# A two-layer block on one core: the last two pairs' down products in halves of 512 tokens, and a buffer of its own for the first weight sums

## The chip, the cores and the metric

One core of a Trainium2 chip runs the whole kernel. Its engines work side by side and meet only at semaphores: TensorE (PE, with its weight loads PEld) multiplies into the eight banks of PSUM, VectorE (DVE) and ScalarE (ACT) read and write PSUM and SBUF, GpSimd (POOL) works in SBUF, and SyncE (SP) starts transfers between SBUF and the chip's memory. The metric is the time of one execution in microseconds, as the median of several runs.

## The reference

Two transformer blocks over `x`, 1024 tokens of 1024 values, all in float32. The change lies in the last part of the second block and in the final norm:

```python
        x = x + merged @ w_out[l]
        h2 = rms_norm(x, norm2[l])
        x = x + jnp.square(jax.nn.relu(h2 @ w_up[l])) @ w_down[l]
    return rms_norm(x, final_norm)
```

`w_up` is 1024 x 4096 and `w_down` 4096 x 1024. `rms_norm` divides each token's values by the root of their mean square (plus 1e-6) and multiplies them by a gain.

## The kernel before

`X` holds the residual, turned: 128 partitions (values), 8 row groups of 128 values, 1024 tokens. A float32 product is made of three matmuls of 512 columns: each operand is split into an upper part (`hi`, rounded) and a rest (`lo`), and hi x hi, lo x hi and hi x lo are added in PSUM. The weights' split is POOL's: one operation makes the upper part by a product with one, a second the rest by subtraction, for 512 columns each (`split_to_slot`, lines 695 and 697).

The MLP runs over 16 pairs (`PAIRS_UP`), each of 256 hidden values. The up product of a pair is made of seven smaller products P1 to P7 over half of the tokens (a Strassen-like scheme: weight blocks and operands are added and subtracted before, results after). POOL makes the sums of weight blocks (`sums`, line 705 by way of `combine`): the sum of two blocks goes to `sum_up`, which lies where `h_hi` and `h_lo`, operands of the layer before, have been. Therefore `sums(0)` waits for `halves_done` at `2 * G_MLP`, the last product of that layer. The order in which POOL makes weights is written out in `W_ORDER`; weight number n goes to slot n mod 4, and POOL waits until the product that used the slot before has been done. After each weight `w_made` is raised by one.

TensorE's order at the start of the MLP is P1 of pair 0, P5 of pair 0, the mean square of `X` by token (`mean_square(4)`, line 797, a product with `mean_w`), P6 of pair 0, P2, P7, the spreading of the roots over the partitions (`spread_rms(4)`), P1 of pair 1, P4, P3, P6 and P5 of pair 1, then the down products of pair 0. SyncE loads pair 1's blocks of `w_up` (lines 562 and 565) once that mean has been made, since the sum of squares `sumsq_m` shares memory with them.

For a pair the hidden values are made in four blocks: VectorE applies relu and the root (`relu`, line 2177), ScalarE squares (line 1545) and makes the upper part (line 1550), VectorE makes the rest (line 2188, raising `hid_ready`). The down product of a pair has eight results q (row groups of `X`) of 1024 tokens: `down` issues 12 matmuls for each (lines 1101 to 1103), two banks wide, and VectorE adds the pair of banks to `X` (`add_down`, line 2200, raising `x_added`). Two pairs of banks alternate. Down weights are loaded in blocks of 256 KB, for two q of one pair each (`load_down`, line 572), into two buffers; a load waits for the split of the block two before it.

The last two pairs, 14 and 15, have their down products made together after the last up product. Each q takes 24 matmuls, those of pair 14 and of pair 15, after `hid_ready` of pair 15. For each q, ScalarE then squares `X` into `sq_f` (line 1194) and multiplies `X` by the final gain in place (line 1582), and VectorE adds the squares up in `sumsq_m` (lines 1614 and 1617). `sumsq_m` lies in memory of `up_1`; the first of these sums waits for the last weight of all, `w_made` at `len(W_ORDER)`:

```python
                if k == 0:
                    if n:
                        dve.wait_ge(w_made, len(W_ORDER))
                    dve.tensor_copy(sums[:], squares[:, 0]).then_inc(summed, 1)
```

VectorE's order there is `add_down(q)`, then the sum for q - 1. After the last q TensorE transposes `X` back to tokens x values (`turn_result`, line 1143, eight transposes for each of the eight blocks of 128 tokens), makes the mean square (`mean_square(5)`), ScalarE takes the root (line 1202), VectorE refines its inverse (lines 1644 to 1655), and VectorE (even blocks, line 2257) and ScalarE (odd blocks, line 1589) write the results, multiplied by the roots, to the four buffers of `y_out`. SyncE stores each block of 512 KB (line 587); a buffer is written again only when its store has been done.

## Time and profile before

| | us |
|---|---|
| median of 3 runs | 2008.71 |
| the runs, lowest and highest | 2003.52, 2009.34 |
| the profiled execution's own time | 2003.49 |
| its span, first to last instruction | 2001.7 |
| busy in it: PE, PEld | 1937.3, 1629.1 |
| busy in it: DVE, POOL, ACT | 942.0, 927.4, 618.9 |

The span is what all the rows count in; 1.8 us lie around it. A busy time says how long an engine had work in flight, not that it set the pace. A matmul's own duration is longer than its share: matmuls are pipelined, and the distance from one start to the next is what counts. "idle before" is the time that an engine stood still just before an instruction, with the instruction that released it.

### The profile page before, as it was taken

Reading aid. Unit: us, or ns where it says so; the run is one execution under the profiler, and the core shown is the slowest. Engines: PE = TensorE matmul, PEld = TensorE weight load, DVE = VectorE, ACT = ScalarE, POOL = GpSimd, SP = SyncE. Lnnn points to the kernel's source line nnn. Section 1 sums busy time; section 2 is a strip of 40 time slices with the busy share of each in tenths; the row PEclk is TensorE's granted clock in tenths of the full one; section 3 lists DMA queues with packets and bytes.
Section 4 is the critical chain, followed back from the end, with each engine's and each line's share of the span. In section 5 each row is a group of like instructions: output and inputs, shape, how many; then the busy total and the mean of one; then the engine's idle time right before and its main releaser. Section 6 shows DMA issues by size and latency. Waiting matters only on the chain.

```text
span 2001.7 us, 27035 instructions
## 1 busy us (share of the span) xinstructions
PE 1937.3 (97%) x9792; PEld 1629.1 (81%) x9792; DVE 942.0 (47%) x1682; ACT 618.9 (31%) x1154; POOL 927.4 (46%) x793
## 2 busy tenths in 40 slices
PE   7999999999999999999999999989999999999987
PEld 6778887788889888888888887878888888888876
DVE  5535554667545544454411216554444444444434
ACT  5025545546344544455300003331111111111123
POOL 4442227623222222112344444486777677776760
PEclk9999999999999999999999999999999999999998
DMA  4411012331111111110111113111121112111102
GB/s 127 106 43 32 27 38 85 87 126 40 41 40 41 30 48 43 32 33 22 32 47 47 48 52 126 58 64 43 44 72 53 43 43 74 53 43 43 53 32 84
DMA packets 145039, 109.85 MB, mean 55 GB/s; under 512 B 11273, under 2 KB 137745, under 8 KB 144929
## 3 DMA queue, kind: packets, MB, share of 16 engines
q1 hardware_dynamic: 132704, 89.67, 15.3%
q10 hardware_dynamic: 12224, 18.70, 3.0%
q8 instruction: 70, 1.15, 0.2%
q14 instruction: 41, 0.33, 0.1%
HBM read 99.91 MB, written 11.59 MB: 56 GB/s over the span
## 4 chain that ended last, share of the span: by engine, by line
PE 87%; DVE 6%; issue 2%; ACT 2%; POOL 1%; DMA 1%; SPq 0%; POOLq 0%; DVEq 0%; ACTq 0%
PE ps L773 12%; PE ps L774 12%; PE ps L775 12%; PE ps L897 6%; PE ps L1101 6%; PE ps L1102 6%; PE ps L1103 6%; PE ps L1062 5%; PE ps L1064 5%; PE ps L1063 5%; PE ps L886 3%; PE ps L872 2%; PE ps L867 1%; PE ps L819 1%; PE ps L821 1%
## 5 line engine op out<-in xcount | busy, mean ns | idle before, releaser
L633 POOL TENSOR_TENSOR w_hi<-raw,ones 128x512 fp32r<-128x512 f32 x146 | 163.7, 1121 | 810.2 <-PE ps L775 794.1
L773 PE MATMUL ps<-h_hi,w_hi 128*128 128x512 f32 x1024 | 407.7, 398 | 12.4 <-DVE tmp L1675 3.4
L774 PE MATMUL ps<-h_lo,w_hi 128*128 128x512 f32 x1024 | 401.5, 392 | 0.0
L775 PE MATMUL ps<-h_hi,w_lo 128*128 128x512 f32 x1024 | 400.8, 391 | 0.0
L2200 DVE TENSOR_TENSOR X<-ps,X 128x1024 f32<-128x1024 f32 x120 | 146.9, 1224 | 230.3 <-PE ps L1103 230.3
L773 PEld LDWEIGHTS ps<-h_hi,w_hi 128*128 128x128 f32 x1024 | 193.7, 189 | 50.8 <-DVE tmp L1675 5.9
L775 PEld LDWEIGHTS ps<-h_hi,w_lo 128*128 128x128 f32 x1024 | 193.2, 189 | 42.1
L774 PEld LDWEIGHTS ps<-h_lo,w_hi 128*128 128x128 f32 x1024 | 193.7, 189 | 34.5 <-issue 0.7
L1101 PE MATMUL ps<-hid_hi,slot_hi 128*128 128x512 f32 x512 | 201.0, 392 | 10.3 <-DVE X L2200 6.8
L637 POOL TENSOR_TENSOR w_lo<-raw,w_hi 128x512 fp32r<-128x512 f32 x146 | 200.8, 1375 | 11.4
L1102 PE MATMUL ps<-hid_lo,slot_hi 128*128 128x512 f32 x512 | 200.4, 391 | 0.0
L1103 PE MATMUL ps<-hid_hi,slot_lo 128*128 128x512 f32 x512 | 200.1, 391 | 0.0
L1545 ACT ACTIVATE ps<-ps 128x512 f32<-128x512 f32 x64 | 37.2, 582 | 515.5 <-DVE ps L2177 515.4
L695 POOL TENSOR_TENSOR slot_hi<-up,ones 128x512 fp32r<-128x512 f32 x96 | 99.9, 1041 | 124.2 <-PE ps L1103 115.8
L897 PEld LDWEIGHTS ps<-v_seq,probs_t 128*128 128x128 f32 x1056 | 136.8, 191 | 15.5 <-DVE o_seq L1747 3.0
L1247 ACT ACTIVATE probs<-probs,least 128x640 f32<-128x640 f32 (+7 forms) x128 | 94.2, 736 | 137.9 <-DVE least L1736 137.6
L897 PE MATMUL ps<-v_seq,probs_t 128*128 128x64 f32 x1056 | 132.2, 269 | 3.1 <-DVE o_seq L1747 1.5
L697 POOL TENSOR_TENSOR slot_lo<-up,slot_hi 128x512 fp32r<-128x512 f32 x96 | 123.8, 1289 | 7.5
L1101 PEld LDWEIGHTS ps<-hid_hi,slot_hi 128*128 128x128 f32 x512 | 96.9, 189 | 31.4 <-DVE X L2200 7.3
L1256 ACT ACTIVATE probs_t<-ps 128x512 f32<-128x512 f32 (+2 forms) x192 | 81.6, 460 | 105.2 <-PE ps L886 104.2
L1103 PEld LDWEIGHTS ps<-hid_hi,slot_lo 128*128 128x128 f32 x512 | 96.9, 189 | 20.3
L1102 PEld LDWEIGHTS ps<-hid_lo,slot_hi 128*128 128x128 f32 x512 | 97.0, 189 | 20.1
(300 smaller groups left out, 3624.3 us busy)
## 6 DMA issues: line engine op xcount, KB each, us to landing
raw<-in_w_in SPq DMA_DIRECT2D x116, 256.0 KB, 2.9
up<-in_w_up SPq DMA_DIRECT2D x32, 512.0 KB, 3.9
down_raw<-in_w_down SPq DMA_DIRECT2D x64, 256.0 KB, 3.4
raw<-in_w_out SPq DMA_DIRECT2D x32, 256.0 KB, 2.8
x_in<-in_x SPq DMA_DIRECT2D x8, 512.0 KB, 7.8
raw_b<-in_w_out SPq DMA_DIRECT2D x16, 256.0 KB, 2.9
x_store<-X ACTq DMA_DIRECT2D x8, 512.0 KB, 2.8
bias_fox<-c_rows ACTq DMA_DIRECT2D x8, 512.0 KB, 4.4
```

The costliest lines, as they stand in the source:

```text
L633: pool.tensor_tensor(w_hi[:, half].rearrange("p k n -> p (k n)"), raw[:, half].rearrange("p k n -> p (k n)"), f32(ones[:, 0:1]).broadcast_ ...
L637: pool.tensor_tensor(w_lo[:, half], raw[:, half], f32(w_hi[:, half]), ALU.subtract).then_inc(weights_split, 1)
L697: pool.tensor_tensor(lo, src, f32(hi), ALU.subtract).then_inc(w_made, 1)
L773: pe.matmul(o, w1, hi[:, k, c], start=first, stop=False)
L774: pe.matmul(o, w1, lo[:, k, c], start=False, stop=False)
L775: mm = pe.matmul(o, w2, hi[:, k, c], start=False, stop=last)
L897: mm = pe.matmul(bank(2, HD), buf["probs_t"][:, (g + gi) % 4, b * P:(b + 1) * P], buf["v"][st][:, kb + b, head * HD:(head + 1) * HD], star ...
L1062: pe.matmul(o, hi[:, k], b_hi[:, k], start=first and k == 0, stop=False, skip_group_check=not first)
L1101: pe.matmul(o, w1, hid[0][:, k, c], start=first and k == 0, stop=False)
L1102: pe.matmul(o, w1, hid[1][:, k, c], start=False, stop=False)
L1103: mm = pe.matmul(o, w2, hid[0][:, k, c], start=False, stop=last and k == 1)
L2200: dve.tensor_tensor(X[:, q], pair(q % 2), X[:, q], ALU.add).then_inc(x_added, 1)
```

## The change

It has two parts.

The start: POOL's sum of two weight blocks for pair 0 goes to `sum_up_0`, memory of its own, and `sums(0)` no longer waits for the last product of the layer before. The upper parts of four weights, P7 of pair 0, P1 of pair 1, P7 and P4 of pair 15, are made by ScalarE (`split_hi`) and not by POOL, which still makes the rests.

The end: the down products of pairs 14 and 15 are made over 512 tokens at a time (`tail`), first all eight q for tokens 0 to 511 (h = 0), then for 512 to 1023 (h = 1), in the order of `tail_order`: three products of pair 14, the same three of pair 15, then both pairs by turns. Each q of a half has one bank. The down weights of both pairs are loaded and split a second time for the second half (blocks E0 to E3). Squares go to a PSUM bank, sums to `sumsq_m`, by halves; the first of them waits for P3 of pair 15. The first half's mean, root, transposes (blocks 0 to 3), scaling and store stand between the second half's products in each engine's order. `y_out` has eight buffers and no waits for a store.

```diff
-    return order + [(f"D{j}", i) for j in range(4) for i in (PAIRS_UP - 2, PAIRS_UP - 1)]
+    a, b = PAIRS_UP - 2, PAIRS_UP - 1
+    order += [("D0", a), ("D1", a), ("D0", b), ("D1", b)]
+    order += [(f"D{j}", i) for j in (2, 3) for i in (a, b)]
+    return order + [(f"E{j}", i) for j in range(4) for i in (a, b)]
+def tail_order():
+    a, b = PAIRS_UP - 2, PAIRS_UP - 1
+    order = [(0, q, i) for i in (a, b) for q in range(3)]
+    order += [(0, q, i) for q in range(3, 8) for i in (a, b)]
+    return order + [(1, q, i) for q in range(8) for i in (a, b)]
+DOWNS = 8 * (PAIRS_UP - 2)
+TAIL_BANK = ((4, 5, 7, 6, 4, 5, 7, 6), (4, 5, 4, 5, 4, 5, 4, 5))
+TAIL_SQUARE = (0, 7)
+TAIL_MEAN = 6
+TURN_PAIR = (0, 1, 0, 1, 0, 1, 2, 3)
+ACT_HI = [("P7", 0), ("P1", 1), ("P7", PAIRS_UP - 1), ("P4", PAIRS_UP - 1)]
+def slot_free(name, i):
+    j = int(name[1])
+    return T_AT[int(name[0] == "E"), 2 * j + 1, i] + 1
+    sum_up_0 = z_at("sum_up_0", W_SLOT, F32, 100)
-    y_out = t_at("y_out", [P, 4, D], F32, 0)
+    y_out = t_at("y_out", [P, NB, D], F32, 0)
...
+                    elif i >= PAIRS_UP - 2:
+                        pool.wait_ge(tail_done, slot_free(name, i))
...
+                if op in ACT_HI:
+                    pool.wait_ge(act_hi_made, ACT_HI.index(op) + 1)
+                else:
+                    pool.tensor_tensor(hi, src, one, ALU.mult).then_inc(slot_hi_made, 1)
+                    pool.wait_ge(slot_hi_made, pool_hi_at(op))
                 pool.tensor_tensor(lo, src, f32(hi), ALU.subtract).then_inc(w_made, 1)
...
-                if i == 0:
-                    pool.wait_ge(halves_done, 2 * G_MLP)
-                combine(sum_up[:], block(i, 2, 1), block(i, 2, 2), ALU.add)
+                total_up = sum_up if i else sum_up_0
+                combine(total_up[:], block(i, 2, 1), block(i, 2, 2), ALU.add)
...
+            def tail(h, q, i):
+                n = W_AT[f"{'DE'[h]}{q // 2}", i]
...
+                last = i + 1 == PAIRS_UP
+                hid, c, o = hid_t[last], (N1, N2)[h], bank(TAIL_BANK[h][q])
+                pe.wait_ge(w_made, n + 1)
+                if last and h == 0 and q == 0:
+                    pe.wait_ge(hid_ready, 4 * PAIRS_UP)
+                if not last:
+                    if h == 0 and q == 0:
+                        pe.wait_ge(r_made, 4 * (PAIRS_UP - 2) + 1)
+                    elif h == 0 and q == 1:
+                        pe.wait_ge(r_made, 4 * (PAIRS_UP - 1) + 1)
+                    elif h == 0 and q == 2:
+                        pe.wait_ge(d_read, 3 * PAIRS_UP)
+                    elif h == 0 and q == 3:
+                        pe.wait_ge(c_read, 2 * PAIRS_UP)
+                    elif h == 0:
+                        pe.wait_ge(x_added, DOWNS + q - 3)
+                    elif q < 2:
+                        pe.wait_ge(x_added, DOWNS + 5 + q)
+                    else:
+                        pe.wait_ge(x_added, DOWNS + 8 + q - 1)
+                for k in range(2):
+                    w1, w2 = hi[:, k, q % 2], lo[:, k, q % 2]
+                    pe.matmul(o, w1, hid[0][:, k, c], start=not last and k == 0, stop=False, skip_group_check=True)
+                    pe.matmul(o, w1, hid[1][:, k, c], start=False, stop=False, skip_group_check=True)
+                    mm = pe.matmul(o, w2, hid[0][:, k, c], start=False, stop=last and k == 1, skip_group_check=True)
+                mm.then_inc(tail_done, 1)
+            def turn_result(i, ks):
+                h = i // 4
+                pe.wait_ge(x_gained, 8 * h + ks[-1] + 1)
+                if i in (2, 3, 4, 5):
+                    pe.wait_ge(y_made[i % 2], (i - 2) // 2 + 1)
...
+            for h, q, i in TAIL:
+                tail(h, q, i)
+                if (h, i) == (1, PAIRS_UP - 1):
+                    if q == 0:
+                        mean_tail(0)
+                    elif 1 <= q <= 4:
+                        turn_result(q - 1, range(KT))
+                    elif q == 6:
+                        turn_result(4, range(6))
+                        turn_result(5, range(6))
+            turn_result(4, [6])
+            turn_result(5, [6])
+            turn_result(4, [7])
+            mean_tail(1)
+            turn_result(5, [7])
+            turn_result(6, range(KT))
+            pe.wait_ge(mean_read, 2)
+            turn_result(7, range(KT))
...
             keep_first(0)
+            act.wait_ge(w_made, W_AT["P6", 0] + 1)
+            split_hi(("P7", 0), up_1[0][:, :, P:2 * P])
+            act.wait_ge(up_1_loaded[1], 16)
+            split_hi(("P1", 1), up_1[1][:, :, 0:P])
...
+            for h in range(2):
+                c = (N1, N2)[h]
+                for q in range(KT):
+                    act.wait_ge(x_added, DOWNS + 8 * h + q + 1)
+                    if q:
+                        act.wait_ge(f_summed, 8 * h + q)
+                    act.activation(bank(TAIL_SQUARE[h]), X[:, q, c], ACT.Square).then_inc(f_squared, 1)
+                    act.activation(X[:, q, c], X[:, q, c], ACT.Copy, scale=gains[:, 4, q:q + 1]).then_inc(x_gained, 1)
...
+                    if h and q in (2, 4):
+                        turn_out(q - 1)
...
+            for h in range(2):
+                for q in range(KT):
+                    add_tail(h, q)
+                    sum_tail(h, q)
+                    if h and q == 0:
+                        root_tail(0)
+                    if h and q in (1, 3):
+                        turn_out(q - 1)
+            root_tail(1)
+            turn_out(4)
+            turn_out(6)
```

`add_tail` adds one bank to 512 tokens of `X`, `sum_tail` adds a bank of squares to `sumsq_m`, `root_tail` is the refinement for four blocks, and `mean_tail` the product with `mean_w` for four. `turn_out(i)` scales block i into `y_out`, on VectorE for even i and on ScalarE for odd. ScalarE makes the two upper parts of pair 15 after the hidden values of pair 14.

## Rows read from the trace of the kernel before

**Rows 1.** The page: busy time, share and instructions of each engine.

```profile
PE 1937.3 (97%) x9792; PEld 1629.1 (81%) x9792; DVE 942.0 (47%) x1682; ACT 618.9 (31%) x1154; POOL 927.4 (46%) x793
```

**Rows 2.** TensorE's waits, 1300 to 2002: waiter <- releaser: total us, times, longest.

```profile
PE ps L1101 <- DVE X L2200: 6.8, 1, 6.8
PE ps L1062 <- POOL slot_lo L697: 5.9, 2, 4.3
PE ps L1101 <- DVE hid_lo L2188: 3.5, 1, 3.5
```

**Rows 3.** Busy time by stage: us, busy (x instructions) by engine, clock, DMA.

```profile
1339.00:1895.00 556.00, 556.00 (x2455) 460.38 (x2454) 249.72 (x282) 67.69 (x117) 413.28 (x353) 1.00 0.16 52
```

**Rows 4.** TensorE's timeline, 1304 to 1335: start, us, instruction, [idle before <-releaser].

```profile
1304.35 0.39 PE L1064 MATMUL ps<-b_hi,slot_lo 128*128 128x512 f32 x1
1309.03 0.80 PE L1062 MATMUL ps<-t_hi,slot_hi 128*128 128x512 f32 x1 [4.30 <-POOL slot_lo L697]
...
1334.08 0.47 PE L1062 MATMUL ps<-t_hi,slot_hi 128*128 128x512 f32 x1 [1.63 <-POOL slot_lo L697]
```

**Rows 5.** POOL's timeline, 1302 to 1309, same columns.

```profile
1302.19 1.29 POOL L705 TENSOR_TENSOR sum_up<-up,up 128x512 f32<-128x512 f32 x1 [3.06 <-PE ps L775]
...
1307.71 1.26 POOL L697 TENSOR_TENSOR slot_lo<-sum_up,slot_hi 128x512 fp32r<-128x512 f32 x1
```

**Rows 6.** The chain that ended last, 1309 to 1320: start us, us, what.

```profile
1309.83 0.43 PE ps L1063
...
1313.38 1.69 PE ps L797 x16
...
1315.09 3.79 DMA up<-in_w_up
```

**Rows 7.** VectorE's and ScalarE's timelines, 1294 to 1308.

```profile
1294.17 0.74 DVE L2116 SCALAR_TENSOR_TENSOR b_lo<-X,gains,b_hi 128x512 fp32r<-128x512 f32 x1
...
1305.24 1.50 DVE L2127 SCALAR_TENSOR_TENSOR b_lo<-X,gains,b_hi 128x512 fp32r<-128x512 f32 x1
...
1307.92 0.68 DVE L2102 TENSOR_TENSOR sumsq_m<-ps,sumsq_m 128x512 f32<-128x512 f32 x1
...
1303.38 0.72 ACT L1522 ACTIVATE b_hi<-X,gains 128x512 fp32r<-128x512 f32 x1 [5.84 <-DVE X L2109]
```

**Rows 8.** The page: groups of POOL's splits, busy us, mean ns | idle before.

```profile
L695 POOL TENSOR_TENSOR slot_hi<-up,ones 128x512 fp32r<-128x512 f32 x96 | 99.9, 1041 | 124.2 <-PE ps L1103 115.8
...
L697 POOL TENSOR_TENSOR slot_lo<-up,slot_hi 128x512 fp32r<-128x512 f32 x96 | 123.8, 1289 | 7.5
```

**Rows 9.** TensorE's, then VectorE's timeline, 1925 to 1957.

```profile
1926.46 0.79 PE L1101 MATMUL ps<-hid_hi,slot_hi 128*128 128x512 f32 x1 [3.49 <-DVE hid_lo L2188]
...
1956.88 0.80 PE L1101 MATMUL ps<-hid_hi,slot_hi 128*128 128x512 f32 x1 [6.84 <-DVE X L2200]
...
1955.00 0.69 DVE L1614 COPY sumsq_m<-sq_f 128x1024 f32<-128x1024 f32 x1 [14.58 <-POOL slot_lo L697]
```

**Rows 10.** Line 572's loads, issue to landing: all 64, then the last six.

```profile
DMA to landing us min/median/max: 2.5/3.4/6.4
...
DMA to landing us min/median/max: 2.5/2.6/2.8
```

**Rows 11.** The chain that ended last, 1980 to 1991.

```profile
1980.63 1.24 DVE X L2200
...
1984.59 1.74 PE ps L797 x16
...
1987.91 2.49 DVE y_out L2257 x2
```

**Rows 12.** DMA engines' busy tenths in 40 slices of 1985 to 2002.

```profile
DMA  0000000000019999999999999999999999992000
```

**Rows 13.** Busy time by stage, in two stretches of transposes.

```profile
1980.60:1984.00 3.40, 2.51 (x21) 2.03 (x19) 3.26 (x3) 2.10 (x2) 0.00 (x0) 1.00 0.00 0
1989.20:1995.60 6.40, 6.29 (x32) 6.05 (x32) 3.40 (x3) 1.94 (x2) 0.00 (x0) 0.58 0.88 351
```

More of the change, by code:

```diff
@@ L581, in _ @@
                         load_down(4 * (i - 1) + j)
-            for n in range(4 * (PAIRS_UP - 2), 4 * PAIRS_UP):
+            for n in range(4 * (PAIRS_UP - 2), len(D_ORDER)):
                 load_down(n)
@@ L724, in _ @@
             sums(0)
-            split_to_slot(("P5", 0), sum_up[:])
+            split_to_slot(("P5", 0), sum_up_0[:])
             split_to_slot(("P6", 0), block(0, 1, 1))
@@ L1087, in first_of_c, with down @@
                 product("P5", i, BANK_C)
-            def down(q, i, hid, first=True, last=True):
+            def down(q, i):
                 n = W_AT[f"D{q // 2}", i]
@@ L1100, in down @@
                         o = bank(2 * (q % 2) + b)
-                        pe.matmul(o, w1, hid[0][:, k, c], start=first and k == 0, stop=False)
-                        pe.matmul(o, w1, hid[1][:, k, c], start=False, stop=False)
-                        mm = pe.matmul(o, w2, hid[0][:, k, c], start=False, stop=last and k == 1)
-                if last:
-                    mm.then_inc(down_done, 1)
+                        pe.matmul(o, w1, hid_t[0][0][:, k, c], start=k == 0, stop=False)
+                        pe.matmul(o, w1, hid_t[0][1][:, k, c], start=False, stop=False)
@@ new lines, in mean_tail @@
+            def mean_tail(h):
+                pe.wait_ge(f_summed, 8 * h + 8)
+                if h:
+                    pe.wait_ge(mean_read, 1)
+                for i in range(4):
+                    b = 4 * h + i
+                    mm = pe.matmul(ps[:, TAIL_MEAN, i:i + 1], sumsq_m[:, b * P:(b + 1) * P], mean_w[:],
+                                   start=True, stop=True)
+                mm.then_inc(mean_done, 1)
+            def turn_result(i, ks):
[3 more added lines that the diff above has]
+                    pe.wait_ge(y_made[i % 2], (i - 2) // 2 + 1)
+                for k in ks:
+                    mm = pe.transpose(ps[:, 2 * TURN_PAIR[i] + k // 4, (k % 4) * P:(k % 4 + 1) * P],
+                                      X[:, k, i * P:(i + 1) * P], ident[:])
+                if ks[-1] == KT - 1:
+                    mm.then_inc(y_turned, 1)
@@ new lines, in root_tail @@
+            def root_tail(h):
+                dve.wait_ge(root_made, 6 + h)
+                ms, root, y, t = (rms[:, n, 4 * h:4 * h + 4] for n in range(4))
+                dve.tensor_scalar(ms, bank(TAIL_MEAN, 4), EPS, None, ALU.add).then_inc(mean_read, 1)
+                dve.wait_ge(mean_read, h + 1)
+                step(dve.reciprocal(y, root))
+                step(dve.tensor_tensor(t, ms, y, ALU.mult))
+                step(dve.tensor_tensor(t, t, y, ALU.mult))
+                step(dve.tensor_scalar(t, t, -0.5, 1.5, ALU.mult, ALU.add))
+                dve.tensor_tensor(y, y, t, ALU.mult).then_inc(scale_ready, 1)
```

138 lines of the change are left out of this document (61 added, 77 removed).

## The prediction

> **What bounds the kernel now.** I read the page first, then TensorE's waits, then the busy table by stages, then each stall's neighbourhood in the timelines and the chain. On the page TensorE is busy for 1937.3 us of the span of 2001.7 us [rows 1], so the change can only win back part of some 64 us and can't make the products shorter. The reader should see in the list of waits that in the last 700 us only three of TensorE's waits are large: 6.8 us on an addition into `X`, 5.9 us on POOL's `slot_lo` (two waits, the longer 4.3) and 3.5 us on `hid_lo` [rows 2]. Between 1339 and 1895 us TensorE is busy for all of 556.00 us, 2455 matmuls at 0.2265 us each [rows 3]: whatever is won before 1339 us is carried unchanged to 1895, and nothing in between can give or take. So two stretches count: the start of the MLP (1302 to 1339) and its end (from 1923). After the last product, at 1980.6, another 21.1 us pass to the span's end [rows 11], in which TensorE only turns results and makes the mean.
>
> **Start of the MLP.** P1 of pair 0 issues its last matmul at 1304.35 and ends 0.23 later, at 1304.6; P5 begins at 1309.03 [rows 4]. It waited for POOL: from the end of P1's split, 1302.19 - 3.06 = 1299.1, POOL idled until the last product of the layer before was done, since `sum_up` lies in `h`'s memory, and only then made three sums and P5's split, 1302.19 to 1308.97 [rows 5]. With `sum_up_0` elsewhere the sums start at 1299.15; the same 6.8 us of work end at 1305.95 (the splits' slots are free at 1302.0, before they are wanted). P5 starts 3.1 us earlier. After the wait of 4.3 us matmuls came 0.43 apart instead of 0.23, the lower of the two clock levels (1.2 against 2.4 GHz), for seven of them [rows 4, 6]: 7 x 0.2 = 1.4 us. After a wait of only 1.63 us the first matmul took 0.47 against 0.80, and the clock had not fallen [rows 4]; the wait that is left is 1.35 us, so the 1.4 us go too. P5 ends at 1308.8, and the mean's sums (last addition 1307.92 + 0.68, [rows 7]) are just ready, so the mean begins 4.6 us earlier than at 1313.38 [rows 6]. What is late next is the load of pair 1, which waits for that mean: 1315.09, landing 3.8 us later, then POOL works without a pause until P6 of pair 1 can begin, at 1334.08 [rows 4, 6]. That chain moves by the 4.6, and by 0.4 more, since ScalarE makes P1's upper half (0.72 for 512 columns [rows 7]) where POOL takes 1.04 and a gap [rows 8]. ScalarE's two new copies stand in front of the `b22` tops, and the first waits there for pair 1's load: tops from 1315.0, the second `b22` rest at about 1318.2, wanted by TensorE at 1318.7. That cover is thin, but a later landing moves POOL's chain by as much, so it is paid once. TensorE reaches P6 of pair 1 at about 1327.9 and starts at 1329.0: **5.0 us won**. Bounds: 3.1 (only the first wait goes) and 5.9 + 1.4 = 7.3 (both waits and the slow clock go whole).
>
> Here a rule speaks against the change. First the row: a VectorE operation with `X` and `b_hi` (both in SBUF) took 1.50 us at 1305.24 with POOL at work, while a like one took 0.74 at 1294.17 without [rows 7]. The Trainium skill (SBUF — State Buffer, Who interferes with whom) states that a VectorE instruction with two SBUF inputs and a GpSimd instruction that reads SBUF exclude one another for their whole length; the trace agrees. By it, POOL's splits moved under VectorE's last operands could hold the mean's sums for one POOL operation, 1.3 us, and the start would gain 3.7 in place of 5.0.
>
> **The end: the wait for the last hidden values.** TensorE ends P3 of pair 15 at 1926.46 - 3.49 = 1923.0 and idles for `hid_lo` [rows 9]. Now three products of pair 14 (18 matmuls, 4.1 us) need no value of pair 15 and fill 1923.0 to 1927.1, past `hid_lo`'s 1926.4. Their banks 4, 5 and 7 are free by 1921. Won: 3.5, and the slow clock after it: its first matmul took 0.79 as at 1309.03 [rows 4, 9], and with eight at 0.2 more that is 1.6. The first block's split is ready in time: POOL gives two upper halves to ScalarE, idle there, and is 2.2 us earlier.
>
> **The end: VectorE behind POOL.** The copy that begins `sumsq_m` waited 14.58 us until POOL had read the last weights, and the addition for the third product stood behind it in VectorE's queue; TensorE idled 6.84 us and restarted at the low clock (first matmul 0.80, again eight) [rows 9]. The new sum waits only for P3 of pair 15. Won: 6.8 + 1.6 = 8.4. The 192 matmuls stay 192, each still with its own weights, at 0.2265 [rows 3]: 43.5 us.
>
> **What is added there.** Eight more loads of 256 KB and eight more splits on POOL. A split is 1.04 + 1.29 and gaps, 2.36 [rows 8]; a load of the last six landed in 2.5 to 2.8 us [rows 10], and waits for the split two before it. So two splits cost 2.65 + 2.36 = 5.0 us and feed 24 matmuls of pairs 14 and 15, 5.4 us: hidden, barely. Following slots block by block, the smallest reserve is 0.4 us (product 4 of the first half) and 0.8 (product 6). At 3.4 us each, the median of all 64 loads, the same reckoning gives 0.3 us of stalls, at 4.0 us 1.5, and at 6.4 us, the largest, 13.9 [rows 10]. I take none: those of over 3 us ran beside loads of `up`, of which none is left here. VectorE adds, ScalarE squares and VectorE sums a product's half in 3 x 0.7 = 2.1 us [rows 7] while TensorE takes 2.72, or 3.8 with a turn: hidden, the first root and four output scalings (1.24 each [rows 11]) too; without that cover each costs its length. Beside the second half TensorE also does 44 transposes (21 took 2.5 [rows 13]: 5.3 us), half of the mean (1.7 / 2 = 0.9 [rows 6]) and six changes of kind and back, estimated at 0.8 from the 0.47 against 0.39 of a first matmul [rows 4]: **7.0 us added on the path**. SyncE issues the stores behind the last loads, about 1955, when the first result is ready; nothing waits for it.
>
> **After the last product.** Before: addition, square, scaling, last transposes, mean (1.74, to 1986.3), root (1.6, to 1987.9), output scaling [rows 11], and eight stores, whose bytes fill 24.5 of the 40 slices of 0.425 us, 10.4 us one behind the other [rows 12]: 21.1 us in all. Now on half the columns: addition, square and sum 0.7 each, last transpose and mean 1.1, root 1.5, first scaling 1.3: 6.0 us to the first of four stores. Then some 0.9 to the first bytes, half of 10.4 = 5.2, and 0.9 to the span's end [rows 12]: 13.0. Won: 8.1.
>
> **Sum.** TensorE's last product ends at 1923.0 + 43.5 + 7.0 = 1973.5 and the span at 1986.5, with the old start; 15.2 us won (by parts 5.1 + 8.4 + 8.1 - 7.0 = 14.6). With the start's 5.0: 20.2. The span becomes 1981.5, an execution like the profiled one 2003.5 - 20.2 = 1983.3. The runs shown spread from 2003.5 to 2009.3 with the median at 2008.7, 5.2 above the profiled one; the same shift on the median gives 1988.5. I take the middle, **1986 us**.
>
> **Rivals.**
> *The start is held by something else* (0.12): VectorE shut out by POOL, or ScalarE held at pair 1's load in front of the `b22` tops. For it speaks the 1.50 us above; against, that the sums are wanted only at 1308.8. Gain 3.1 to 3.7 there: 1988.
> *The weight feed runs late* (0.12): loads land in 4 us rather than 2.6. It speaks for it that the reserve is 0.4 us, against it that the six loads without company took 2.6 [rows 10]. 1.5 us of stalls, up to 3 with a slow restart: 1988 to 1989.
> *Turning locks TensorE to the copies* (0.1): results 2 to 5 reuse two pairs of banks and wait for an output scaling of 1.24 us [rows 11]. Each scaling stands behind an addition and a sum in VectorE's queue; if all four waits last one scaling, 5 us: 1991. Against it, a product and its turn give VectorE 3.8 us.
> *It doesn't overlap* (0.04): a wait that I misread keeps the first half's norm behind the second half; then the 8.1 and part of the 8.4 stay unearned and 7.0 is added: 1999 to 2006.
> *Slower: the clock* (0.03). Between 1989.2 and 1995.6 TensorE did 32 transposes with the granted clock at 0.58 [rows 13]. If turns between products drop the second half to the low level, each matmul costs 0.2 us more; 20.2 / 0.2 = 101 matmuls is where the change turns slower, and only the second half's 96 with some of the mean and turns beside them reach it: 2009 to 2012. Against it: 21 transposes between 1980.6 and 1984.0 with short idle left it at 1.00 [rows 13]. The Trainium skill (TensorE: Matmul & The Clock Gate, Loop structure matters more than you think) warns of waits between matmuls that send the clock down; by it turns with nothing idle around them should be harmless, and rows 13 agree.
>
> **How the numbers follow.** Forecast 0.59, the rest as given. A measurement tells 0.3%, 6 us, from no change. Faster holds the forecast, the first three rivals and a little of the fourth: 0.93; same 0.04; slower 0.03. The range goes from 1979 (both waits at the start gone whole, executions like the profiled one, and a shorter end) to 1997 (turning and feed together on the median): 8 in 10.
>
> **What would show it.** P5 of pair 0 starts 1.3 us after P1 and P6 of pair 1 about 5 us earlier. From P3 of pair 15 to the last product about 50.5 us (before 57.6), with no wait over 1 us and a clock near 1.00; from it to the end about 13 (before 21.1). A stall before product 4 or 6 of the first half names the feed; matmuls 0.43 apart name the clock. I am wrong if the stretch 1339 to 1895 has changed, or if POOL, not TensorE, ends the first half.

## The result, and the profile after

| | before | after |
|---|---|---|
| median of 4 runs each, us | 2007.63 | 1985.9 |
| the runs, lowest and highest | 2003.52, 2009.34 | 1985.52, 1987.36 |
| the profiled execution's own time | 2003.49 | 1987.36 |
| its span | 2001.7 | 1985.6 |

The ratio of after to before is 0.9896, with a 95% interval from 0.9879 to 0.9913: the change makes the kernel 21.7 us faster. The forecast was 1986.

TensorE's waits of the changed kernel, from 1290 us to the end (waiter, releaser, total us, times, longest), answer to [rows 2]:

```profile
PE ps L1094 <- POOL slot_lo L730: 2.3, 2, 1.2
PE ps L1188 <- ACT X L1683: 1.8, 1, 1.8
PE ps L1094 <- DVE u_t L2249: 0.8, 1, 0.8
```

The waits of 6.8 us on the addition into `X` and of 3.5 us on `hid_lo` are gone, and the 5.9 us on `slot_lo` are 2.3. What is left are 1.10 us before P5 of pair 0 and 1.22 us before P6 of pair 1. New is 1.8 us behind the last product, where TensorE turns the last values; the 0.8 us on `u_t` stood in before too. TensorE's timeline at these places, which answers to [rows 4], and POOL's, which answers to [rows 5]:

```profile
1310.08 0.50 PE L1094 MATMUL ps<-t_hi,slot_hi 128*128 128x512 f32 x1 [1.10 <-POOL slot_lo L730]
...
1333.39 0.47 PE L1094 MATMUL ps<-t_hi,slot_hi 128*128 128x512 f32 x1 [1.22 <-POOL slot_lo L730]
```

```profile
1302.09 1.29 POOL L730 TENSOR_TENSOR slot_lo<-up,slot_hi 128x512 fp32r<-128x512 f32 x1
1303.52 1.29 POOL L738 TENSOR_TENSOR sum_up<-up,up 128x512 f32<-128x512 f32 x1
...
1308.76 1.27 POOL L730 TENSOR_TENSOR slot_lo<-sum_up,slot_hi 128x512 fp32r<-128x512 f32 x1
1309.98 1.49 POOL L728 TENSOR_TENSOR slot_hi<-up,ones 128x512 fp32r<-128x512 f32 x1
```

POOL's first sum follows the split of P1 by 0.1 us; before, POOL stood still for 3.06 us there. Neither wait brought the clock down: the first matmuls took 0.50 and 0.47 us and those behind them came 0.23 apart. The table by stretches (us, then busy time and instructions of PE, PEld, DVE, ACT, POOL, then the granted clock, the DMA share and GB/s) has the middle of the MLP, the start, the second half's products, and the turns behind the last product:

```profile
1339.00:1890.00 551.00, 551.00 (x2433) 456.39 (x2432) 248.38 (x280) 67.80 (x117) 410.11 (x349) 1.00 0.16 52
1310.00:1316.00 6.00, 5.92 (x34) 5.20 (x35) 4.63 (x11) 1.99 (x6) 5.04 (x5) 1.00 0.03 8
1947.10:1972.00 24.90, 24.90 (x136) 21.04 (x136) 14.55 (x23) 10.88 (x17) 11.58 (x10) 1.00 0.35 128
1975.70:1979.60 3.90, 3.76 (x18) 3.36 (x17) 3.33 (x8) 1.42 (x3) 0.00 (x0) 0.50 0.06 23
```

The middle is what it was [rows 3]: busy for all of its 551.00 us, 2433 matmuls at 0.2265 us. The second half's products and the turns between them keep TensorE busy for all of 24.90 us at a clock of 1.00.

Since the middle can't change, each kernel below is read by three distances: from the start of P1 of pair 0 to the end of P3 of pair 15 (start and middle), from there to the end of the last down product (the tail), and from there to the span's end. The first two kernels:

```
                       P1 at     P1 to P3   tail    behind it   their sum
before                 1301.85   620.96     57.62   21.27       699.85
after                  1306.10   616.03     49.66   13.81       679.50
```

The changed part is 4.9 + 8.0 + 7.5 = 20.4 us shorter, and the span only 16.1, because this execution reached P1 of pair 0 4.25 us later than that of before. Up to there both kernels run the same code. 2.8 of the 4.25 us come from the first 60 us (same columns as above, first before, then after):

```profile
0.00:60.00 60.00, 48.15 (x220) 39.87 (x221) 35.47 (x45) 29.66 (x37) 26.21 (x42) 0.94 0.42 121
```

```profile
0.00:60.00 60.00, 47.22 (x208) 39.20 (x209) 32.31 (x42) 29.61 (x37) 22.61 (x41) 0.89 0.38 111
```

While the first inputs land, after got through 208 matmuls and before through 220, with a granted clock of 0.89 against 0.94. The other 1.4 us arise between 304 and 447 us. Over the fourteen profiled executions of this study P1 of pair 0 began between 1300.28 and 1306.10 us. Whole runs scatter by about as much; where only the order of work at the start or the end of the MLP differs, the three distances say more than the medians.

### The profile page after: what moved, and what is told of

Read it like the earlier page. It is cut to its first block, busy times and chain, and to the rows that moved or that the text cites. A ratio compares the mean times of both kernels' runs of the same rounds, so it can differ in the third digit from the quotient of the medians.

```text
span 1985.6 us, 27160 instructions
## 1 busy us (share of the span) xinstructions
PE 1935.4 (97%) x9792; PEld 1628.3 (82%) x9792; DVE 947.4 (48%) x1704; ACT 624.3 (31%) x1175; POOL 942.5 (47%) x805
## 3 DMA queue, kind: packets, MB, share of 16 engines
q1 hardware_dynamic: 134880, 91.77, 15.8%
## 4 chain that ended last, share of the span: by engine, by line
PE 89%; DVE 6%; issue 2%; ACT 2%; POOL 1%; DMA 0%; SPq 0%; DVEq 0%; ACTq 0%; POOLq 0%
PE ps L805 12%; PE ps L806 12%; PE ps L807 12%; PE ps L929 6%; PE ps L1135 5%; PE ps L1133 5%; PE ps L1134 5%; PE ps L1094 5%; PE ps L1096 5%; PE ps L1095 5%; PE ps L918 3%; PE ps L904 2%; PE ps L851 1%; PE ps L899 1%; PE ps L853 1%
## 5 line engine op out<-in xcount | busy, mean ns | idle before, releaser
L2292 DVE TENSOR_TENSOR X<-ps,X 128x1024 f32<-128x1024 f32 x112 | 137.2, 1225 | 205.3 <-PE ps L1135 205.3
L1133 PE MATMUL ps<-hid_hi,slot_hi 128*128 128x512 f32 x448 | 174.3, 389 | 0.0
L1134 PE MATMUL ps<-hid_lo,slot_hi 128*128 128x512 f32 x448 | 174.3, 389 | 0.0
L1135 PE MATMUL ps<-hid_hi,slot_lo 128*128 128x512 f32 x448 | 174.3, 389 | 0.0
L730 POOL TENSOR_TENSOR slot_lo<-up,slot_hi 128x512 fp32r<-128x512 f32 x96 | 123.7, 1290 | 10.0 <-ACT slot_hi L1643 2.8
L1835 DVE RECIPROCAL inv_total<-total 128x1 f32<-128x1 f32 x192 | 31.4, 163 | 154.1 <-PE ps L929 152.2
L1094 PE MATMUL ps<-t_hi,slot_hi 128*128 128x512 f32 x256 | 100.0, 391 | 3.1 <-POOL slot_lo L730 2.3
L1095 PE MATMUL ps<-t_lo,slot_hi 128*128 128x512 f32 x256 | 99.6, 389 | 0.0
```

The source lines that it names most:

```text
L1094: pe.matmul(o, hi[:, k], b_hi[:, k], start=first and k == 0, stop=False, skip_group_check=not first)
L1095: pe.matmul(o, hi[:, k], b_lo[:, k], start=False, stop=False, skip_group_check=not first)
L1133: pe.matmul(o, w1, hid_t[0][0][:, k, c], start=k == 0, stop=False)
L1134: pe.matmul(o, w1, hid_t[0][1][:, k, c], start=False, stop=False)
L1135: mm = pe.matmul(o, w2, hid_t[0][0][:, k, c], start=False, stop=k == 1)
L2292: dve.tensor_tensor(X[:, q], pair(q % 2), X[:, q], ALU.add).then_inc(x_added, 1)
```

## The experiments

None of these kernels leaves work out. Distances in us come from one profiled execution each, medians from the runs; "won" means against before.

### The start alone

The changes at the start, put into the kernel before:

```diff
-                if i == 0:
-                    pool.wait_ge(halves_done, 2 * G_MLP)
-                combine(sum_up[:], block(i, 2, 1), block(i, 2, 2), ALU.add)
+                total_up = sum_up if i else sum_up_0
+                combine(total_up[:], block(i, 2, 1), block(i, 2, 2), ALU.add)
...
+ACT_HI = [("P7", 0), ("P1", 1)]
```

> The kernel before with the start of the change alone: sum_up_0, and the upper parts of P7 of pair 0 and P1 of pair 1 by ScalarE. Theory (TensorE's path through sums, mean, load of pair 1 and POOL): from P1's last matmul of pair 0 to P6 of pair 1 it takes 24.5 us where before took 29.7, so 5.0 us less than before in all, 2002.6 where before is 2007.6. Rival (VectorE shut out by POOL, or ScalarE held at the load): 3.1 to 3.7 us less. The second wait, before P6 of pair 1, about 1.2 us by the theory.

Measured: 2002.29 us (1999.3 to 2003.87), ratio 0.9974 [0.9965, 0.9984]. The distances are 616.10, 58.13 and 21.28. The start won 4.86 us, as in the whole change (4.93), and nothing behind it gave any of it back: the two waits of the tail are still 3.49 and 6.85 us.

What did change is the price of the clock behind the wait of 3.49 us. TensorE's timeline of this kernel (start, us, instruction, idle before):

```profile
1925.54 0.50 PE L1114 MATMUL ps<-hid_hi,slot_hi 128*128 128x512 f32 x1 [3.49 <-DVE hid_lo L2211]
...
1926.12 0.41 PE L1116 MATMUL ps<-hid_hi,slot_lo 128*128 128x512 f32 x1
1926.34 0.61 PE L1114 MATMUL ps<-hid_hi,slot_hi 128*128 128x512 f32 x1
1926.76 0.63 PE L1115 MATMUL ps<-hid_lo,slot_hi 128*128 128x512 f32 x1
```

In before the first matmul behind that wait was already slow, 0.79 us [rows 9]. Here, behind the same wait, the first four start 0.34, 0.24 and 0.22 us apart, and only then do they come 0.42 apart.

Without ScalarE's two copies, with `sum_up_0` alone:

> The kernel before with sum_up_0 alone; POOL makes all upper parts. Theory: the first wait falls from 4.3 to about 1.1 us and the slow clock goes; the mean moves by 4.6 us and the load of pair 1 with it, so 4.6 us less than before, and the wait before P6 of pair 1 is 1.5 us. Rival (ScalarE's two copies carry more than 0.4 us of the start's gain): 3 us or less.

Measured: 2002.67 us (1999.41 to 2005.08), ratio 0.9982 [0.9972, 0.9991]; 616.33, 59.15 and 21.31. Its waits at the start, and those of the kernel with the copies:

```profile
PE ps L1062 <- POOL slot_lo L698: 2.6, 2, 1.5
```

```profile
PE ps L1075 <- POOL slot_lo L711: 2.4, 2, 1.3
```

The buffer is worth 4.6 us, ScalarE's copies 0.23 us more. The medians of the two kernels, 0.4 us apart with runs over some 5 us, can't tell them apart; the waits, 1.53 and 1.28 us before P6 of pair 1, can.

### One wait of the end

The kernel before, with only the wait in front of the first sum of squares changed:

```diff
-                        dve.wait_ge(w_made, len(W_ORDER))
+                        dve.wait_ge(w_made, W_AT["P3", PAIRS_UP - 1] + 1)
```

> The kernel before with one wait changed: the first sum of squares waits for P3 of pair 15 and no longer for the last weight. The down products keep their 1024 tokens. Theory: the wait of 6.8 us goes and with it the slow restart, 8.4 us less than before; the wait of 3.5 us for hid_lo stays, POOL's splits are ready 3 us or more before they are wanted. Rival (the next wait in line takes its place, a split that waits for its slot): 3 to 5 us less, with a wait of 3 us or more on slot_lo.

Measured: 1997.38 us (1996.1 to 1998.68), ratio 0.9957 [0.994, 0.9973]. The distances are 622.56, 47.31 and 21.29. One line in VectorE's queue shortens the tail by 10.3 us. TensorE's waits and its restart:

```profile
PE ps L1062 <- POOL slot_lo L697: 6.0, 2, 4.3
PE ps L1101 <- DVE hid_lo L2188: 3.5, 1, 3.5
```

```profile
1929.35 0.50 PE L1101 MATMUL ps<-hid_hi,slot_hi 128*128 128x512 f32 x1 [3.49 <-DVE hid_lo L2188]
1929.68 0.39 PE L1102 MATMUL ps<-hid_lo,slot_hi 128*128 128x512 f32 x1
1929.92 0.39 PE L1103 MATMUL ps<-hid_hi,slot_lo 128*128 128x512 f32 x1
```

The 6.84 us are gone with what followed them, and this time the other wait, of the same 3.49 us, cost no clock at all: the tail is 47.31 = 43.5 (192 matmuls) + 3.49 + 0.3. The 0.3 is what a restart costs even at full clock. By the same subtraction before paid 57.62 - 43.5 - 10.33 = 3.8 us for two restarts, the start alone 4.3 and the buffer alone 5.3; less 0.3 for each restart, the two low clocks cost 3.2, 3.7 and 4.7.

At the start this kernel has the old wait of 4.3 us. Its windows behind that wait and over the tail, and the window of before behind its own:

```profile
1310.30:1318.00 7.70, 7.68 (x29) 6.52 (x30) 1.10 (x2) 0.07 (x1) 6.78 (x6) 0.59 0.01 3
1925.80:1973.00 47.20, 43.71 (x193) 36.11 (x193) 17.51 (x17) 15.94 (x17) 15.28 (x12) 1.00 0.09 29
```

```profile
1309.00:1315.10 6.10, 6.07 (x29) 5.26 (x30) 1.11 (x2) 0.01 (x1) 5.87 (x6) 0.76 0.01 4
```

The same 29 matmuls took 6.1 us in before and 7.7 us here: the clock stayed low for all twelve matmuls of P5 and part of the mean, where in before it came back after seven. `end_only`, below, is like this one. So the execution from which the prediction was made had a mild low clock at the start, and 620.96 is the smallest of the three values with that wait.

### The end alone

The whole change at the end, with the old `sum_up`, its wait, and no copies at the start:

```diff
-ACT_HI = [("P7", 0), ("P1", 1), ("P7", PAIRS_UP - 1), ("P4", PAIRS_UP - 1)]
+ACT_HI = [("P7", PAIRS_UP - 1), ("P4", PAIRS_UP - 1)]
...
+                if i == 0:
+                    pool.wait_ge(halves_done, 2 * G_MLP)
```

> The changed kernel with the start as before: sum_up and its wait, POOL makes the upper parts of pair 0 and of P1 of pair 1. Theory: the two parts of the change don't touch each other, so the end alone is worth the whole less the start: 15.2 us by the sum, 15 to 17 by the measured whole of 21.7 less 5. The stretch from P3 of pair 15 to the last product takes 49.7 us as in the changed kernel. Rival (the parts share a gain): 19 us or more.

Measured: 1990.42 us (1986.95 to 1992.65), ratio 0.9916 [0.9898, 0.9934]; 622.20, 49.66 and 13.41. The tail is to the hundredth that of the whole change, so the parts don't touch each other. From P3 of pair 15 to the span's end it takes 63.1 us where before took 78.9: the end alone is worth 15.8. Against this kernel the start is worth 622.20 - 616.03 = 6.2 us.

### How much are the halves worth?

`one_wait` is one line; the halves with their second feed, norm and stores are most of the diff. The start (as in the first kernel) and that one line (as in the third) together, still with 1024 tokens to a product:

> The kernel before with the start of the change and the one changed wait, 1024 tokens at a time. Theory: 5.0 + 8.4 = 13.4 us less than before, so that the halves of 512 tokens with all that goes with them are worth the other 7 to 8. Rival: if the halves only serve to take that wait away, this kernel is as fast as the changed one, 21 us less.

Measured: 1991.75 us (1990.38 to 1992.98), ratio 0.9925 [0.9908, 0.9941]; 616.11, 48.95 and 21.32, in sum 686.4. The whole change has 679.5. So of its 20.4 us the start gives 4.9, the one line 8.7 to 10.3, depending on the clock behind the other wait, and the halves the last 6.9. In the tail the halves are even longer (49.66 against 48.95, with the 3.5 us of wait filled and the turns added); they earn their part behind the last product, where half of the norm and of the stores is left.

### Turns between the products, or behind them

Turns and stores of the first half's blocks moved behind the last product, and with them the twelve turns of blocks 4 and 5; the sums, the mean and the root of the first half are left where they are:

```diff
-                    elif 1 <= q <= 4:
-                        turn_result(q - 1, range(KT))
-                    elif q == 6:
-                        turn_result(4, range(6))
-                        turn_result(5, range(6))
```

> The changed kernel with the first half's four turns, scalings and stores moved behind the last product; its sums and its root stay beside the second half. Theory (what is beside the products costs TensorE 4.1 us there and takes the same from the end, since eight stores at 10.4 us then set the end): within 2 us of the changed kernel either way; the last product ends 4 us earlier, and 17 to 18 us follow it instead of 13.6. Rival (the hidden stores are what the halves bring): 5 us slower or more.

Measured: 1984.15 us (1983.78 to 1985.38), ratio 0.9889 [0.9873, 0.9906]; 616.00, 44.70 and 16.26. The tail lost 4.96 us and the rest grew by 2.45 against after: in sum 677.0 against 679.5. The 44 transposes with their changes of kind cost 0.113 us each on TensorE's path, near the 0.12 of [rows 13]; what they bring is less. Behind the last product it was forecast that 17 to 18 us would follow, and 16.3 did. The transfers of this kernel from 1966 to 1983 (busy share of the DMA engines in 40 slices of 0.425 us, tenths):

```profile
DMA  0000000000799999999999999999999999800000
```

and those of after from 1969 to 1986:

```profile
DMA  0000000000000000000000005999999999996000
```

Eight stores take 25 slices, 10.6 us, and four take 13, 5.5 us. But in after the first bytes leave 7.4 us behind the last product and here 4.2 us; these first stores need nothing of the second norm. 5.1 us more of transfers, less 3.2 us of earlier start, and some 0.5 between them and the span's ends make the 2.45; the turns had cost twice that. The medians of the two kernels can't tell them apart (the intervals overlap), the distances do: with `after_again` (679.0, below) the gain is 2.0 us, with after 2.5.

Only the twelve turns of the second half's own blocks moved, from beside product 6 to behind the loop:

```diff
-                    elif q == 6:
-                        turn_result(4, range(6))
-                        turn_result(5, range(6))
+            turn_result(4, range(6))
+            turn_result(5, range(6))
```

> The changed kernel with twelve transposes of blocks 4 and 5 moved from before the last product to behind it, where TensorE waits 1.8 us for the last scaled values. Theory: 1.3 to 1.5 us less than the changed kernel, the last product ends that much earlier and still 13.6 us follow it. Rival (they delay the last transposes and the mean): no change, or up to 0.5 us more.

Measured: 1981.37 us (1980.11 to 1983.94), ratio 0.9878 [0.9861, 0.9894]; 616.18, 48.31 and 13.16. The tail is 1.35 us shorter and the rest doesn't grow: these turns fit into the 1.84 us for which TensorE waits there for the last values.

The same, with the squares' sums in memory of `rstd` instead of `up_1`, so that pair 1's load waits for no mean:

```diff
-    sumsq_m = z_at("sumsq_m", [P, S], F32, 102)
+    sumsq_m = rstd
...
-                    sp.wait_ge(mean_done, 5)
```

The first of those sums then waits for the last root of pair 15 (`r_made`) and no longer for P3.

> As turn_in_gap, and the sum of squares lies in rstd's memory instead of in that of up_1, so the load of pair 1 no longer waits for the mean. Theory: the wait of 1.2 us before P6 of pair 1 goes, since POOL's splits no longer wait for that load; 2.4 to 2.7 us less than the changed kernel. Rival (POOL is the bound there anyway, or a new wait of ScalarE): the 1.2 us stay, and it equals turn_in_gap.

Measured: 1983.4 us (1981.27 to 1983.99), ratio 0.9881 [0.9864, 0.9897]; 614.64, 48.31 and 13.22. TensorE's waits:

```profile
PE ps L1093 <- POOL slot_lo L729: 1.1, 1, 1.1
PE ps L1093 <- DVE u_t L2247: 0.8, 1, 0.8
PE ps L1187 <- ACT X L1681: 0.5, 1, 0.5
```

The wait before P6 of pair 1 is gone and 1.5 us with it. Pair 1's load was issued 0.2 us after P1 of pair 0 began, and 8.7 us after it in the changed kernel, so the mean held that load, as the prediction said. The median is not below that of the kernel before it (1981.37); this execution reached P1 of pair 0 at 1305.83 and the other at 1300.75, and by the distances it is 676.2 against 677.7.

### The order of the first products

Pairs 14 and 15 by turns from the start, without the three products of pair 14 in front:

```diff
-    order = [(0, q, i) for i in (a, b) for q in range(3)]
-    order += [(0, q, i) for q in range(3, 8) for i in (a, b)]
+    order = [(0, q, i) for q in range(8) for i in (a, b)]
```

> The changed kernel with the first half's products in plain turns, pair 14 then pair 15 for each q, and not three of pair 14 first. Theory: TensorE waits for hid_lo after one product instead of none: 3.5 - 1.4 = 2.1 us of wait, and no slow clock after so short a wait, so 2.1 us more on the way from P3 of pair 15 to the last product (49.7). Rival (the clock falls as after 3.5 us): 3.7 us more.

Measured: one run, 1988.22 us (before beside it: 2007.85); 616.08, 52.21 and 13.20. The timeline:

```profile
1924.73 0.47 PE L1164 MATMUL ps<-hid_hi,slot_hi 128*128 128x512 f32 x1 [2.23 <-DVE hid_lo L2279]
1925.04 0.40 PE L1165 MATMUL ps<-hid_lo,slot_hi 128*128 128x512 f32 x1
```

One product of pair 14, six matmuls or 1.36 us, still stands in front, and 3.49 less 1.36 is about the 2.23 of this wait. The tail is 2.55 us longer by it, and after it the clock did not fall.

### How thin is the weight feed?

One more POOL operation, a sum of `sum_up` with itself, before the split that product 4 of the first half wants:

```diff
+                if D_ORDER[n] == ("D2", PAIRS_UP - 1):
+                    pool.wait_ge(tail_done, slot_free("D1", PAIRS_UP - 2))
+                    combine(sum_up[:], sum_up[:], sum_up[:], ALU.add)
```

> The changed kernel with one more POOL operation of 1.3 us just before the split of block D2 of pair 15, on which product 4 of the first half waits. Theory (that reserve is 0.1 to 0.4 us): a wait of 1.0 to 1.3 us on slot_lo before the second part of product 4, of which nothing is caught up: the way from P3 of pair 15 to the last product grows from 49.7 by about 1.1 us. Rival (the reserve is larger than it looks, since TensorE's queue runs ahead): no wait.

Measured: one run, 1986.94 us; 616.08, 50.69 and 13.25. Its waits:

```profile
PE ps L1097 <- POOL slot_lo L730: 2.4, 2, 1.3
PE ps L1191 <- ACT X L1686: 1.8, 1, 1.8
PE ps L1168 <- POOL slot_lo L730: 0.9, 1, 0.9
```

The added sum and the second part of product 4 in the timelines:

```profile
1931.02 1.04 POOL L738 TENSOR_TENSOR sum_up<-sum_up 128x512 f32<-128x512 f32 x1 [4.33 <-PE ps L1170]
...
1934.58 0.50 PE L1168 MATMUL ps<-hid_hi,slot_hi 128*128 128x512 f32 x1 [0.93 <-POOL slot_lo L730]
```

The same place in the changed kernel as it is:

```profile
1933.08 1.30 POOL L730 TENSOR_TENSOR slot_lo<-down_raw,slot_hi 128x512 fp32r<-128x512 f32 x1
...
1934.14 0.39 PE L1167 MATMUL ps<-hid_hi,slot_lo 128*128 128x512 f32 x1
1934.43 0.50 PE L1165 MATMUL ps<-hid_hi,slot_hi 128*128 128x512 f32 x1
```

Counted from the end of P3 of pair 15, the added sum of 1.04 us makes this split end 1.02 us later than in after, the product's second part begins 1.02 us later, and the tail is 1.03 us longer. Nothing of the delay was absorbed, so the reserve at product 4 is none. The lines of after say the same: the split ends at 1934.38, and the product begins at 1934.43, 0.06 us late and with the slower first step of a restart, 0.17 us in all. The forecast had worked out a reserve of 0.4.

### The changed kernel again, and a better one

The changed kernel as it is, beside the next one on the same chip:

> The changed kernel once more, beside two_late and on its chip. Theory (what differs between executions of one kernel lies ahead of the MLP, in the loads of x and the first clock changes): P1 of pair 0 begins anywhere from 1300 to 1306 us, from there to the end of P3 of pair 15 it takes 616.0 to 616.2 again, the last products 49.7 and the rest 13.2 to 13.8; 1984 to 1988 in all. Rival (the end varies as much): one of the last three differs by over 1 us.

Measured: 1984.93 us (1983.8 to 1986.17), ratio 0.9899 [0.9883, 0.9916]; 616.13, 49.66 and 13.20. Start, middle and tail are those of after within 0.1 us. Only the stretch behind the last product differs, by 0.6 us, and the reason stands in the chains of work. First after, from its last wait on (start, us, what):

```profile
1974.02 0.33 PE ps L1188
1974.35 1.39 PE ps L1177 x8
...
1975.73 3.74 PE ps L1188 x17
```

then the second execution:

```profile
1971.03 0.33 PE ps L1188
1971.36 0.82 PE ps L1177 x8
```

Behind the same wait of 1.84 us the eight small matmuls of the mean took 1.39 us in the one and 0.82 in the other. The clock had fallen in after (0.50 in the window above) and not here.

The best that the distances point to: sums in `rstd` as above, only blocks 0 and 1 turned and stored beside the second half, blocks 2 and 3 turned behind the last product and in front of the second mean, and the rest behind that.

```diff
-                    elif 1 <= q <= 4:
+                    elif 1 <= q <= 2:
                         turn_result(q - 1, range(KT))
-                    elif q == 6:
-                        turn_result(4, range(6))
-                        turn_result(5, range(6))
+            turn_result(2, range(KT))
+            turn_result(3, range(KT))
             mean_tail(1)
```

> As both_more (sum of squares in rstd's memory), but blocks 0 and 1 are turned and stored beside the second half and blocks 2 and 3 behind the last product, with blocks 4 to 7 after them. Theory (TensorE's time before the last product and the stores' time after it should be level): the last products take 46.9 us, and 13.1 follow if the clock stays up in the turns, 1.5 us less in all than both_more. Rival (turns at the low clock, 0.22 us each, set the end): up to 15.9 follow, 1.3 us more than both_more.

Measured: 1978.34 us (1976.84 to 1980.94), ratio 0.9869 [0.9852, 0.9885]; 614.68, 46.50 and 13.54, in sum 674.7. All its runs lie below all those of the changed kernel beside it (from 1983.8), and the distances are 4.3 us shorter: 1.5 at the start and 3.2 in the tail, less 0.3 behind it. In the tail 28 transposes fewer stand on TensorE's path, 28 x 0.113 = 3.2, and what they leave to be done behind it lies beside the second norm.

## Why the prediction was right, by its own steps

**What bounds.** The stretch 1339 to 1895 runs at 0.2265 us a matmul in before and after, and what was won before it is there behind it: the tails of `end_only` and of after agree to 0.01 us with starts that differ by 6.2.

**Start, 5.0 us.** 4.9 in the profiles of before and after. The wait before P5 was 1.10 (forecast 1.35) and that before P6 of pair 1 1.22 (forecast 1.1). The copies on ScalarE, put at 0.4, gave 0.23. The term for the clock, 1.4, was the price of the one execution that was read; in the two other kernels with the wait of 4.3 us (`one_wait` and `end_only`), P1 to P3 was 622.56 and 622.20, so that the start is worth 4.9 to 6.5, inside the bounds of 3.1 to 7.3. That each of those three kernels paid, and none with a wait of 1.1 to 1.5 us, is what the step needed.

**The held start** (0.12) did not come, though its cause is there. VectorE's operation on `X` and `b_hi` again took longer beside POOL's split, and POOL's next upper half too:

```profile
1308.87 0.69 DVE L2194 TENSOR_TENSOR sumsq_m<-ps,sumsq_m 128x512 f32<-128x512 f32 x1 [0.49 <-ACT ps L1579]
1309.48 1.09 DVE L2219 SCALAR_TENSOR_TENSOR b_lo<-X,gains,b_hi 128x512 fp32r<-128x512 f32 x1
```

The second took 1.09 us where 0.74 is its like [rows 7], and POOL's upper half at 1309.98 took 1.49 where it mostly takes 1.04 [rows 8]. It was paid by engines for which nobody waited: P5 began with POOL's split, and the mean followed without a wait. So 5.0 was right and the 3.7 that the prediction had worked out for this rival was not. The Trainium skill (SBUF — State Buffer, Who interferes with whom) states the exclusion, and these longer operations agree with it; its price lay beside the path.

**Filling the wait for `hid_lo`, 3.5 + 1.6.** The 3.5 went. `plain_order` shows it from the other side: with one product of pair 14 in front instead of three, 2.23 us of it came back. The 1.6 for the clock is the term with the least support: behind this same wait one execution paid nothing, and the two low clocks together cost 3.2 us in before, as forecast, and up to 4.7 in others. The forecast left out the 0.3 of each restart, and that is why its parts, 14.6, fall short by 0.6 of the 15.2 that it took.

**VectorE behind POOL, 8.4.** Shown alone by `one_wait`: the tail 10.3 us shorter, 6.84 for the wait and 3.5 for clocks and one restart. That is more than 8.4 because here the other wait's low clock failed to come as well.

**Added on TensorE's path, 7.0.** The tail is 49.66, and 192 matmuls are 43.5, so 6.2 were added. By `turn_late` the 44 transposes with their changes of kind came to 4.96 (forecast 5.3 and most of 0.8), which leaves 1.2: 0.90 for the half mean with the restart behind it (forecast 0.9), 0.17 for the late split at product 4, and 0.1 that stays open. The tail was forecast at 50.5.

**The weight feed.** No wait for it stands in the list, POOL waited for loads by 0.5 us at most, and the loads of the tail landed in 2.6 us at the median, so the rival of a late feed (0.12) fell. But the reserve of 0.4 us at product 4 was not there. Two products' 2.72 us less the split's 2.36 give that figure. In after POOL, which stood waiting for the slot, began that split at 1931.96, 0.31 us after TensorE had gone on from the product that frees the slot (1931.65); with the split's own 2.42 us and 0.05 to TensorE that makes 2.78, so it came 0.06 us late. It is the slot that sets this place, not a load. **Turning locks TensorE** (0.1) fell: no wait on an output scaling in the list. **It doesn't overlap** and **slower by the clock** fell with the window from 1947.1 to 1972.0: 136 matmul records, no idle time, clock 1.00, with the root, the scalings and the stores of the first half beside them. The Trainium skill (TensorE: Matmul & The Clock Gate, Loop structure matters more than you think) warns of idle between matmuls, of which there was none here, and the window agrees. That turns are harmless as such does not follow: the second line of [rows 13] has 32 of them with 6.29 of 6.40 us busy at 0.58, and in after the last 17 ran at 0.50 with 3.76 of 3.90 us busy. Both stretches stand behind waits, of 1.19 and 1.84 us.

**Behind the last product, 8.1 won.** 7.5 in after, 7.9 to 8.1 in `end_only`, `after_again` and `turn_in_gap`; the 0.6 that after lacks is the mean at the low clock. The step forecast addition, square, scaling and the mean as they came: 0.70, 0.60, 0.65 and then 0.33 + 1.39 or 0.82 in the chain of work.

**The number itself.** The sum was 20.2 and the distances say 20.4. Part of that closeness is luck: the tail gave 8.0 where 7.1 was forecast (57.6 to 50.5), and the stretch behind the last product 7.5 where 8.1 was, and the two errors nearly cancel. What was added to it, the middle between the profiled execution and the median, was a choice about scatter and not about the change. On the medians the difference is 21.7: the time expected from the median before, 2008.7 - 20.2 = 1988.5, was 2.6 too high. 1.1 of them are the median of before, 2007.63 with the new run; the other 1.5 fit to the profiled before, which paid less for its clocks than its likes did (620.96 against 622.2 and 622.6, 57.6 against 58.1 and 59.2).

**What it missed.** That the turns beside the products are a loss was open to the same sums: 44 transposes cost 5.0 us on the path, and earlier stores can earn only what the strip of transfers has in excess of the norm that it covers. The prediction priced both sides and never set them against each other. `turn_late`, `turn_in_gap` and `two_late` do: by the distances 2.0, 1.3 and (without its 1.5 at the start) 2.8 us below `after_again`. Of these three only `two_late` is also apart from it in its runs.

## What to carry to other kernels

Look behind a wait for what queues after it on the same engine: one wait put too late in VectorE's order, for memory that was free far earlier, cost 9 to 10 us, more than all the rest of the work on the end won (6.9), and one line mends it. Before work is moved beside the bounding engine's products, ask whether any of it runs on that engine: what other engines did beside TensorE's products was free here, and what TensorE itself did between them cost its full length. And when a change is local, measure distances between fixed points inside the trace; they repeated to 0.1 us where whole runs scattered by several, except where the clock behind a wait differed (0.6 us behind the last product).

## What was not expected of the hardware

- **The clock after a wait is not a fixed price.** Behind the same 3.49 us of idle TensorE the matmuls came at full pace for all of the tail (`one_wait`), for five (`start_one_wait`) or three (`start_only`) matmuls and then at 0.42 us, or were slow from the first (before, 0.79 us). Behind the 4.3 us at the start seven matmuls were slow in before, and all twelve and part of the mean in `one_wait` and `end_only`. Behind the same 1.84 us the clock fell in after (0.50 while the last 17 transposes ran, 3.74 us) and did not in `after_again`, with the same code; the eight small matmuls took 1.39 us in after, 1.05 in `end_only`, and 0.82 in `after_again`, `plain_order` and `pool_delay`. A wait of 2.23 us, and those of 1.1 to 1.7 at the start, cost no clock. What decides between them isn't visible in these traces and stays open.
- **Tiny operations are caught by POOL too.** The first half's root is made on VectorE beside POOL's splits. Four values to a partition:

```profile
1949.56 0.16 DVE L2363 TENSOR_TENSOR rms<-rms 128x4 f32<-128x4 f32 x1
1949.76 0.97 DVE L2364 TENSOR_TENSOR rms<-rms 128x4 f32<-128x4 f32 x1
1950.76 0.17 DVE L2365 TENSOR_SCALAR rms<-rms 128x4 f32<-128x4 f32 x1
1950.97 1.12 DVE L2366 TENSOR_TENSOR rms<-rms 128x4 f32<-128x4 f32 x1
```

  POOL's operations at that time:

```profile
1949.67 1.04 POOL L728 TENSOR_TENSOR slot_hi<-down_raw,ones 128x512 fp32r<-128x512 f32 x1
1950.79 1.28 POOL L730 TENSOR_TENSOR slot_lo<-down_raw,slot_hi 128x512 fp32r<-128x512 f32 x1
```

  L2364 and L2366 took 0.16 us each for the second half, at 1976.67 and 1977.08, with POOL idle. Both have two inputs from SBUF, began just after a POOL operation did, and ended within 0.02 us of its end. The third operation of that kind (L2363, 0.16) began only as a POOL operation was ending, and those with one input (0.17) did not grow. Here it was hidden; on a path of many small steps each of them could cost a microsecond.
- **The first microseconds of the kernel scatter most.** With the same code P1 of pair 0 began between 1300.28 and 1306.10 us. Most of it is there early: the first matmul of `diag_hi` began between 50.3 and 55.6 us. From there to P1 it took 1249.0 to 1251.7 us, so the rest scatters too, by up to 2.8.
